# A two-layer decoder trunk in split float32: the moving columns of the long products taken in pairs from the two halves of a tile

## What is computed

```python
def reference(x, p, ...):
    for layer in range(2):
        h = rmsnorm(x, norm_g[layer, 0])
        if layer == 0:
            x = x + rwkv7_time_mix(h, ...)      # r, k, v, gates: h' @ w; then a recurrence; then y @ w_rkvo[3]
        else:
            k, v = shared_kv(x, ...)            # 2 products 1024 x 1024
            x = x + diff_attention(h, k, v, ...)  # h @ w_q, attention, o @ w_o
        x = x + square(relu(rmsnorm(x, g1) @ w1)) @ w2     # w1 1024 x 4096, w2 4096 x 1024
        x = x + (p[layer] @ w_up) * sigmoid(rmsnorm(x, g2) @ w_gate)
    return x
```

## Time and profile before

| | us |
|---|---|
| median of 3 runs | 1489.94 |
| lowest, highest | 1488.85, 1491.85 |
| the profiled execution, its own time | 1489.34 |
| its span, first to last instruction | 1487.2 |
| PE busy | 1431.5 |
| PEld busy | 1147.8 |
| DVE, ACT, POOL busy | 681.5, 583.1, 548.5 |

### The profile page before, as it was taken

The page is one execution under the profiler, slowest core; times in us unless marked ns, Lnnn a source line. Parts: engine busy times, 40 slices in busy tenths (PEclk is TensorE's granted clock), DMA queues, the critical chain, the costliest instruction groups (busy, mean ns, idle before and its releaser), DMA issues.

```text
span 1487.2 us, 23258 instructions
## 1 busy us (share of the span) xinstructions
PE 1431.5 (96%) x9043; PEld 1147.8 (77%) x9043; DVE 681.5 (46%) x1116; ACT 583.1 (39%) x924; POOL 548.5 (37%) x311
## 2 busy tenths in 40 slices
PE   6999998789999999999999999999999999999998
PEld 5777877666888888888878777666888888888877
DVE  6799978566443101331148443276544101340153
ACT  6785436454422212222254432485422221232252
POOL 3130012216344533535332333345353534435342
PEclk9999999999999999999999999999999999999999
DMA  6212100311323232232232422200223232232321
GB/s 195 85 57 86 57 2 4 122 31 35 109 85 105 93 127 85 85 113 86 100 107 85 142 86 85 85 1 30 85 85 113 86 127 85 85 113 86 111 87 57
DMA packets 119900, 126.43 MB, mean 85 GB/s; under 512 B 6268, under 2 KB 114556, under 8 KB 119816
## 3 DMA queue, kind: packets, MB, share of 16 engines
q1 hardware_dynamic: 119120, 123.99, 25.5%
q0 software_dynamic: 320, 0.66, 0.2%
q10 hardware_dynamic: 376, 0.61, 0.2%
HBM read 123.12 MB, written 2.12 MB: 84 GB/s over the span
## 4 chain that ended last, share of the span: by engine, by line
PE 86%; DVE 5%; ACT 4%; issue 3%; POOL 1%; DMA 1%; SPq 0%; ACTq 0%; DVEq 0%; POOLq 0%
PE pb L618 25%; PE pb L620 24%; PE pb L619 24%; PE pb L1341 1%; PE pb L1309 1%; PE pb L748 1%; PE pb L1311 1%; PE pb L1310 1%; ACT whi L1468 1%; PE pb L1368 1%; DMA xtok<-in_x_dram 1%; PE pb L1350 1%; ACT KV L1714 1%; POOL wlo L514 0%; PE pb L811 0%
## 5 line engine op out<-in xcount | busy, mean ns | idle before, releaser
L511 POOL TENSOR_TENSOR wlo<-wraw,whi 128x1024 fp32r<-128x1024 f32 x96 | 230.0, 2396 | 675.8 <-ACT whi L1468 660.8
L618 PE MATMUL pb<-xh,whi 128*128 128x512 f32 x1088 | 429.1, 394 | 3.4 <-DVE xl L2098 1.3
L619 PE MATMUL pb<-xl,whi 128*128 128x512 f32 x1088 | 424.3, 390 | 0.0
L620 PE MATMUL pb<-xh,wlo 128*128 128x512 f32 x1088 | 424.1, 390 | 0.0
L1468 ACT ACTIVATE whi<-wraw 128x2048 fp32r<-128x2048 f32 x108 | 206.2, 1909 | 242.3 <-PE pb L620 238.9
L618 PEld LDWEIGHTS pb<-xh,whi 128*128 128x128 f32 x1088 | 204.5, 188 | 61.7 <-issue 17.3
L620 PEld LDWEIGHTS pb<-xh,wlo 128*128 128x128 f32 x1088 | 204.7, 188 | 43.0
L619 PEld LDWEIGHTS pb<-xl,whi 128*128 128x128 f32 x1088 | 204.7, 188 | 42.4 <-issue 1.0
L514 POOL TENSOR_TENSOR wlo<-wraw,whi 128x1024 fp32r<-128x1024 f32 x96 | 234.9, 2447 | 0.0
L618 PE MATMUL pb<-hid_h,whi 128*128 128x512 f32 x512 | 199.3, 389 | 0.0
L619 PE MATMUL pb<-hid_l,whi 128*128 128x512 f32 x512 | 199.2, 389 | 0.0
(11 more groups left out here) (323 smaller groups left out, 1768.3 us busy)
## 6 DMA issues: line engine op xcount, KB each, us to landing
wraw<-in_mlp_w_dram SPq DMA_DIRECT2D x128, 512.0 KB, 4.3
wraw<-in_rwkv_w_rkvo_dram SPq DMA_DIRECT2D x32, 512.0 KB, 4.4
wraw<-in_ple_w_gate_dram SPq DMA_DIRECT2D x16, 512.0 KB, 4.4
xtok<-in_x_dram SPq DMA_DIRECT2D x8, 512.0 KB, 6.4
wraw<-in_diff_w_q_dram SPq DMA_DIRECT2D x8, 512.0 KB, 4.0
wraw<-in_w_k_shared_dram SPq DMA_DIRECT2D x8, 512.0 KB, 4.3
wraw<-in_w_v_shared_dram SPq DMA_DIRECT2D x8, 512.0 KB, 4.3
wraw<-in_diff_w_o_dram SPq DMA_DIRECT2D x8, 512.0 KB, 4.0
```

Source lines behind the costliest of these rows:

```text
L511: pool.tensor_tensor(wlo[:, par, front], wraw[:, par, front], whi[:, par, front].bitcast(F32), ALU.subtract)
L618: mm(o, wh, ah, start=first, stop=False)
L619: mm(o, wh, al, start=False, stop=False)
L620: return mm(o, wl, ah, start=False, stop=last)
```

## The change

`three` gets a helper, `woven`, which gives a tile of 512 columns in another order: two columns from the first half, two from the second, two from the first, and so on (0, 1, 256, 257, 2, 3, 258, 259, ...). The two moving operands and the output are taken through it. Column by column, each sum lands at the address where it landed before, so nothing outside `three` changes. As an access of one partition, a run of 512 words becomes 128 steps of 2 words x 2 halves, 256 words apart, x 2 words in a row.

```diff
             mm = pe.matmul
 
+            def woven(t):
+
+                return t.rearrange("p (a b c) -> p b a c", a=2, c=2)
+
             def three(o, n, w, xs, first, last):
 
-                (wh, wl), (ah, al) = w, xs
+                (wh, wl), (ah, al) = w, (woven(t) for t in xs)
+                o = woven(o)
                 mm(o, wh, ah, start=first, stop=False)
                 mm(o, wh, al, start=False, stop=False)
                 return mm(o, wl, ah, start=False, stop=last)
```

## The result

| | us |
|---|---|
| before, median of 4 runs | 1490.15 (1488.85 to 1491.85) |
| after, median of 4 runs | 2000.71 (1999.91 to 2006.46) |
| ratio | 1.3434, 95% interval 1.3405 to 1.3462 |
| span of the profiled execution, before and after | 1487.2 and 1999.1 |

A forecast was written before the change was run, and what follows sets the result against it. TensorE was taken to bound the kernel. 5088 matmuls x 213.3 ns = 1085.3 us, plus 5.1 for the odd start, minus 7.3 of waits and 2.1 at 1.2 GHz, gave +1081 on 1489.3: 2570 us, range 1486 to 2667 us.

The forecast's parts named there:

- The bound: TensorE is busy 96% of the span; what the 5088 edited matmuls in `three` cost goes nearly whole into the time.
- The price of a new piece: Moving operand read: each new small piece of memory takes two slots, 1.67 ns, inferred from TensorE's stepped weight loads.
- The number of new pieces: Each woven matmul's 256 two-word runs all count as new pieces: 426.7 ns, 440.0 from start to start, +213.3.
- (c): Rival: half of the second visits find their 16 bytes open; 192 new pieces, +107 ns a matmul, 2032 us; chance 0.06.
- (a): Rival: pairs are free, the port holding a piece of each stream open; matmuls stay at 226.7 ns, 1490 us; chance 0.36.
- (b): Rival: pairs are dearer, as in weight loads beside running matmuls; 383 ns more per matmul, 3435 us; chance 0.07.
- (d): Rival: faster, alternation spreads accesses over more memory and the 13.3 ns that are no columns vanish; 1422 us; chance 0.03.
- The range: Whole kernel, 1486 to 2667 us; the upper end takes 1.74 ns a run, +232 ns for each of 5088 matmuls.
- The odd start: First 24 matmuls read from word 3; woven pairs straddle 16-byte boundaries, 213 ns more each, 653 ns apart, 5 us together.
- The writes: Woven output to PSUM, whole pairs at an even word: taken as 0 extra, bounded by the read side's figures.
- The fixed 13.3 ns: Part of a contiguous matmul's 226.6 ns at full clock beyond its columns' 213.3; kept and added to the woven matmul.

## Why the prediction was wrong, point by point

- **The bound.** Right: the edited lines are on the path throughout, and 5088 times the difference of one matmul gives the whole.
- **The price of a new piece.** Right in the main. I took 1.667 ns from the stepped weight loads, whose own numbers were 1.74 to 2.33 ns; the moving port has 452 / 256 = 1.77 ns (pairs by 16 bytes), and 1.69 to 1.95 for other steps. That it comes so near is partly luck: the four loads of a group start within 0.02 us of each other (L1277 of before, at 842.79 to 842.81 us), so their durations don't isolate one column. The rule of the Trainium skill ("Advanced Engine Details and Errata", "Memory Cachelines") that two hits on a line absorb its latency doesn't hold here: pairs by 16 bytes, two hits each, take 452 ns where a contiguous run takes 227. At 1.2 GHz it nearly holds: 453 against 427 ns for pairs by 16 bytes, and 427 for the woven order.
- **The number of new pieces.** This is the term that failed. "256 x 1.667 = 426.7 ns" took every run for a new piece. Half of the runs return to one of two pieces that are still open and cost about one slot: 128 x 1.667 + 128 x 0.833 = 320 ns, +107 ns and not +213; measured +102 to +104. Where four streams leave no piece open on return, the forecast number comes out: 2574 us against 2570. The prediction named this as its own sign of being wrong, a port that holds two pieces open.
- **The rivals.** (c) had 320 ns a matmul and 2032 us; measured 2001. The number is right and the cause near, the count is luck: (c) let half of the returns find their piece open at no cost and the rest pay in full, 192 x 1.667; what the runs fit is that all of them find it open and pay half, which is the same sum. I had given it 0.06, because I saw it as a halfway house between two clean cases and had read the profile's rows for the price alone, not for how many pieces a port keeps. (a), (b) and (d) fell by the time itself; but the first reason that (a) gave, a piece of each stream held open, is what the two fixed pairs show (217 ns). What (a) missed is that a return isn't free between openings.
- **The range.** Its upper end, by the terms it names, comes to 1489.3 + 1180 + 5 - 7 - 2 = 2665 us and not 2667; nothing hangs on that.
- **The odd start.** Wrong: 330 ns, not 653. Pieces count once, however pairs straddle them.
- **The writes.** Right at 0. Of the two sentences of the Trainium skill on PSUM in that section, the one on pairs agrees with the run (0.9996), the one on any order that isn't contiguous doesn't.
- **The fixed 13.3 ns.** I kept them as no matter of the memory. One pair read over and over takes 215 ns (median; 219 in the mean) where a contiguous run takes 227, so 8 to 12 of them are. They shouldn't have been added to the 426.7.

## What to carry to other kernels

The moving operand of a float32r matmul at full clock has no slack: 16 bytes are opened in 1.77 ns, a little more than the 1.67 in which their four words are used. Orders that took only 8 of them before hopping cost 1.34 to 1.76 times in this kernel. If a hop can't be avoided, take whole aligned pieces, and as many in a row as possible (runs of 64 words cost 1 to 3 ns a matmul). The output could be written to PSUM in aligned pairs hopping by 1 KiB for nothing, so such a permutation is better placed there than in the read; single words and other distances weren't measured by themselves. To price an order of addresses, count the pieces it opens and the returns to one of the last two, and not the runs.

## What the runs showed of the hardware that I had not expected

TensorE's moving port keeps two 16-byte pieces open, and not four: two pairs in turn cost 217 ns per 512 columns wherever they lie (16 bytes to 1 KiB apart), four in turn 451 to 574 ns (medians). A read that stays in one piece is faster than a contiguous one, 215 against 227 ns. And the time of an order without returns doesn't follow TensorE's clock: pairs by 16 bytes take 453 ns at 1.2 GHz and 452 at 2.4.
